# Finishing the prompt's rows inside the expert loop instead of behind it (hybrid decoder step, one core)

## The reference, cut to what matters

```python
g_idx = top_k(softmax(t @ rw1 + rb1), 1)               # one of 4 groups
v2, e_idx = top_k(logits of the 4 experts in it, 2)    # two of its experts
gates = one_hot(4 * g_idx + e_idx) * softmax(v2) * p_top
hid = silu(t @ w_gate[e]) * (t @ w_up[e]) * gates
out = sum over the two experts of hid @ w_down[e]      # hidden width 256
x = x + g2 * out                                       # x: the residual row
y = x * rsqrt(mean(x * x) + EPS) * final_norm_g        # both groups
```

## Time and profile before

| | us |
|---|---|
| median of 3 runs (1165.39 to 1166.51) | 1165.52 |
| the profiled execution's own time | 1166.91 |
| its span | 1165.1 |
| PE busy in it | 1075.8 (92%) |
| POOL busy in it | 312.9 (27%) |
| mean granted clock of TensorE | 0.974 |

### The profile page before, as it was taken

One profiled execution on the slowest core, in us unless ns is written; L12 is line 12 of the kernel. 1 busy time (PEld: TensorE's weight loads), 2 busy tenths in 40 slices (PEclk: granted clock), 3 DMA queues, 4 the chain that ended last, 5 costly groups with the idle time before them and its releaser, 6 DMA issues. The chain is left out here.

```text
span 1165.1 us, 18015 instructions
## 1 busy us (share of the span) xinstructions
PE 1075.8 (92%) x5413; PEld 806.9 (69%) x5414; DVE 765.8 (66%) x1256; ACT 516.1 (44%) x732; POOL 312.9 (27%) x370
## 2 busy tenths in 40 slices
PE   3799999999797989999999989999999999999992
PEld 2357777776465668787787646888888788888860
DVE  5557475747579954378887788555777555555375
ACT  5134252422333225446665243544566455544373
POOL 0046272626141000030000003333334433333244
PEclk9799999999989999999999999999999999999996
DMA  9933656567774459386766557897799877775597
GB/s 281 316 109 101 190 158 198 154 180 246 222 156 162 137 160 250 148 226 215 248 222 217 163 217 253 238 294 216 216 272 271 219 212 220 222 208 113 111 358 306
DMA packets 165460, 244.75 MB, mean 210 GB/s; under 512 B 65327, under 2 KB 122831, under 8 KB 161255
## 3 DMA queue, kind: packets, MB, share of 16 engines
q1 hardware_dynamic: 135065, 167.54, 45.0%
q0 software_dynamic: 17040, 57.87, 19.0%
q10 hardware_dynamic: 13302, 18.66, 4.6%
HBM read 169.36 MB, written 75.84 MB: 210 GB/s over the span
## 5 line engine op out<-in xcount | busy, mean ns | idle before, releaser
L126 PE MATMUL experts_psGU<-weights_we_hi,experts_x_hi 128*128 (+1 forms) x344 | 141.2, 410 | 2.1 <-DVE experts_x_lo L2714 1.0
L128 PE MATMUL experts_psGU<-weights_we_lo,experts_x_hi 128*128 (+1 forms) x344 | 136.0, 395 | 0.0
L127 PE MATMUL experts_psGU<-weights_we_hi,experts_x_lo 128*128 (+1 forms) x344 | 136.0, 395 | 0.0
L2540 POOL DMA_INDIRECT acc_d<-experts_o_sb,experts_to_col x40 | 71.0, 1776 | 209.2 <-DMA acc_d<-experts_o_sb,experts_to_col 109.5
L126 PE MATMUL front_psM<-front_hT_hi,front_w_hi 128*128 128x512 f32 x256 | 106.7, 417 | 0.9 <-DVE front_hT_lo L1043 0.9
L127 PE MATMUL front_psM<-front_hT_hi,front_w_lo 128*128 128x512 f32 x256 | 101.7, 397 | 0.0
L2733 DVE TENSOR_TENSOR experts_o_sb<-experts_psD,experts_g2r 128x1024 f32<-128x1024 f32 x43 | 52.7, 1225 | 74.5 <-PE experts_psD L128 74.5
L128 PE MATMUL front_psM<-front_hT_lo,front_w_hi 128*128 128x512 f32 x256 | 101.2, 395 | 0.0
L126 PEld LDWEIGHTS experts_psGU<-weights_we_hi,experts_x_hi 128*128 128x128 f32 x344 | 64.7, 188 | 20.9 <-issue 6.4
L128 PEld LDWEIGHTS experts_psGU<-weights_we_lo,experts_x_hi 128*128 128x128 f32 x344 | 64.6, 188 | 15.7
L2704 DVE TENSOR_TENSOR weights_we_lo<-weights_we_raw,weights_we_hi (+1 forms) x64 | 75.5, 1220 | 0.0
(11 more groups left out here) (530 smaller groups left out, 2522.3 us busy)
## 6 DMA issues: line engine op xcount, KB each, us to landing
front_raw<-in_w_ada SPq DMA_DIRECT2D x24, 1024.0 KB, 14.2
weights_we_raw<-in_exp_w_gate SPq DMA_DIRECT2D x16, 1024.0 KB
weights_we_raw<-in_exp_w_up SPq DMA_DIRECT2D x16, 1024.0 KB
weights_wd_raw<-in_exp_w_down SPq DMA_DIRECT2D x16, 1024.0 KB
front_xraw<-in_x_prompt SPq DMA_DIRECT2D x4, 2048.0 KB, 10.9
part_d<-middle_ev ACTq DMA_DIRECT2D x16, 512.0 KB, 3.8
middle_xt<-in_x_prompt SPq DMA_DIRECT2D x16, 512.0 KB, 4.8
middle_part<-part_d SPq DMA_DIRECT2D x16, 512.0 KB, 5.6
```

Source lines behind the costliest of these rows:

```text
L126: pe.matmul(out, l_hi, r_hi, start=start, stop=False)
L127: pe.matmul(out, l_lo, r_hi, start=False, stop=False)
L128: return pe.matmul(out, l_hi, r_lo, start=False, stop=stop)
L2540: pool.indirect_dma_start(acc_d, bass.IndirectOffsetOnAxis(tc[:, u, :], 0), osb[:, u, :], None, compute_op=ALU.add).then_inc(added, 16)
```

## The change

**Last slots are marked.** Routing gives a slot's gate a negative sign where it is the row's last: nine small POOL operations form the signs, DVE waits for them (`signs`), and after the sort takes the sign off again into `R.last`. POOL then builds `R.rows`, four indices per slot: the row to fetch, the row to add to (out of bounds for a last slot of the prompt), the row to fetch a sum from and the row to store to (both out of bounds for every other slot, and for padding).

**POOL's step.** Its order is new: `sums(t-4)` (the scatter-add without last slots, and behind it a gather-add from `acc_d` onto `osb` for last slots only), then `gather(t)`, then `store(t-6)`, which stores finished rows to the output, then waits for the transfers of the iteration before, `columns` (copies the next four indices), and `power(t-4)`, which raises the mean square to -0.5.

**ACT and DVE.** ACT gets `row_squares(s-2)` in each step, ahead of the weight splits. DVE gets `root_step(s-3)`, three operations on 128x1 that refine the power, and `row_norm(s-3)`, 128x1024. `g2r` has one buffer instead of two.

**Behind the loop** the 8 pairs of blocks, their loads and stores and the flags for them are gone; three late tiles and the samples are left, and some of their sums move from PE to DVE.

The diff, cut to its core:

```diff
-    def gather(self, pool, R, h2_d, t, u):
-        pool.tensor_copy(self.ic[:, u, :], R.idx[:, bass.ds(t, 1)]).then_inc(self.ic_ok, 1)
-        pool.wait_ge(self.ic_ok, t + 1)
-        pool.sem_inc(self.fence, 1)
-        pool.indirect_dma_start(self.xg[:, u, :], None, h2_d, bass.IndirectOffsetOnAxis(self.ic[:, u, :], 0)
+    def columns(self, pool, R, t, u):
+        pool.tensor_copy(self.cols[:, u, :], R.rows[:, bass.ds(t, 1), :].rearrange("p a n -> p (a n)")).then_inc(self.ic_ok, 1)
+    def gather(self, pool, h2_d, t, u):
+        pool.indirect_dma_start(self.xg[:, u, :], None, h2_d, bass.IndirectOffsetOnAxis(self.cols[:, u, 0:1], 0)
                                 ).then_inc(self.xg_in[u], 16)
...
+                if j == 0:
+                    dve.wait_ge(signs, 9)
                 gated = dve.tensor_tensor(A[:, 1, r], A[:, 0, r], b2(gt[:], NCOL), ALU.mult)
...
+            def sums(t, u):
+                pool.wait_ge(oev, OEV0 + t + 1)
+                pool.sem_inc(fence, 1)
+                if not isinstance(t, int) or t:
+                    pool.wait_ge(added, 16 * t)
+                    pool.sem_inc(freed, 1)
+                pool.sem_inc(fence, 1)
+                pool.indirect_dma_start(acc_d, bass.IndirectOffsetOnAxis(W.cols[:, u, 1:2], 0), osb[:, u, :], None,
+                                        bounds_check=TOK - 1, oob_is_err=False, compute_op=ALU.add).then_inc(added, 16)
+                pool.indirect_dma_start(osb[:, u, :], None, acc_d, bass.IndirectOffsetOnAxis(W.cols[:, u, 2:3], 0),
+                                        bounds_check=TP - 1, oob_is_err=False, compute_op=ALU.add).then_inc(acc_in[u], 16)
+            def power(t, u):
+                pool.wait_ge(mean_ok, MEAN0 + t)
+                pool.sem_inc(fence, 1)
+                pool.tensor_tensor(fss[:, u, 2:3], fss[:, u, 1:2], half[:], ALU.pow).then_inc(powers, 1)
+            def store(t, u, to):
+                pool.wait_ge(normed, NORM0 + t + 3)
...
             with pool.Fori(6, last + 1, 2) as t:
                 for d in range(2):
+                    pool.wait_ge(W.ic_ok, t + d + 1)
+                    pool.sem_inc(fence, 1)
+                    sums(t + d - 4, d)
                     pool.wait_ge(xt_ps, t + d - 1)
-                    W.gather(pool, R, h2_d, t + d, d)
-                    scatter(t + d - 4, d)
+                    pool.sem_inc(fence, 1)
+                    W.gather(pool, h2_d, t + d, d)
+                    store(t + d - 6, d, W.cols[:, d, 3:4])
+                    n, v = t + d - 1, 1 - d
+                    pool.wait_ge(xg_in[v], 8 * n + 16 - 8 * v)
...
+                    W.columns(pool, R, n + 2, v)
+                    power(t + d - 4, d)
...
+            def row_squares(t, u):
+                act.wait_ge(acc_in[u], 8 * t - 8 * u + 16 + ACC0)
...
+                act.activation(junk[:], osb[:, u, :], ACT.Square, scale=1.0 / 32, accum_out=fss[:, u, 0:1]).then_inc(fsq, 1)
+                act.wait_ge(fsq, FSQ0 + t + 3)
+                act.activation(fss[:, u, 1:2], fss[:, u, 0:1], ACT.Identity, bias=eps[:]).then_inc(mean_ok, 1)
...
+            def row_norm(t, u):
+                dve.wait_ge(fstep, STEPS * t + 2 * STEPS + 3)
+                dve.wait_ge(y_out[u], 8 * t - 8 * u + YOUT0)
+                dve.scalar_tensor_tensor(out=fo[:, u, :], in0=osb[:, u, :], scalar=fss[:, u, 5:6], in1=F.gn[:],
+                                         op0=ALU.mult, op1=ALU.mult).then_inc(normed, 1)
```

More of the change, by code:

```diff
@@ L2422, in experts @@
         SHARED = [(1, 0), (2, 0), (2, 1)]
-        PAIR = 2 * D * 4
-        homes = [(n, i * PAIR) for n in ("we_raw", "we_hi") for i in range(ROW_PAIRS // 2)]
-        rows = [k.over(f"rows{g}", [P, 2, D], homes[g][0], F32, homes[g][1]) for g in range(ROW_PAIRS)]
+        g2s = k.over("g2s", [TS, D], "we_raw")
         fix = k.over("late_rows", [P, LATE, D], "wd_raw")
@@ L2543, in expert_pool @@
             for t in range(2, 6):
+                W.columns(pool, R, t, t % 2)
+                pool.wait_ge(W.ic_ok, t + 1)
+                if t >= 4:
+                    sums(t - 4, t % 2)
                 pool.wait_ge(xt_ps, t - 1)
-                W.gather(pool, R, h2_d, t, t % 2)
+                W.gather(pool, h2_d, t, t % 2)
                 if t >= 4:
-                    scatter(t - 4, t % 2)
+                    power(t - 4, t % 2)
+                if t < 5:
+                    pool.wait_ge(xg_in[1 - t % 2], 8 * (t - 1) + 16 - 8 * (1 - t % 2))
@@ L2565, in expert_pool @@
                                         ).then_inc(late_in[d], 16)
+            store(end - 2, 0, last_to[:, 0, :])
             pool.wait_ge(late_in[0], 16)
@@ L2631, in squares @@
+            def squares(n):
+                if n == LATE_A:
+                    act.wait_ge(fsq, FSQ0 + end + 2)
+                if n < LATE_C:
+                    act.wait_ge(own_sum, n + 1)
+                elif n == LATE_C:
+                    act.wait_ge(c_sum, 1)
                 else:
                     act.wait_ge(s_x3, 1)
-                for r, x in enumerate(unit(n)):
-                    if r not in blocks:
-                        continue
-                    if n != ORDER[0] or r:
-                        act.wait_ge(sq, SQ[n] - len(unit(n)) + r)
-                    act.activation(junk[0:x.shape[0], :], x, ACT.Square, accum_out=part(n, 0)[:, r:r + 1]).then_inc(sq, 1)
+                if n:
+                    act.wait_ge(sq, n)
+                x = unit(n)
+                act.activation(junk[0:x.shape[0], :], x, ACT.Square, accum_out=part(n, 0)).then_inc(sq, 1)
@@ L2664, in expert_act @@
                     silu(s, u)
-                    gate_rows(s - 1, 1 - u)
+                    gate_rows(s - 1)
+                    row_squares(s - 2, u)
                     with act.If((code & 1) > 0):
@@ L2676, in expert_act @@
             silu(end + 1, 1)
-            gate_rows(end, 0)
+            gate_rows(end)
+            row_squares(end - 1, 1)
             with act.If((code & 1) > 0):
@@ L2683, in expert_act @@
             hidden_hi(end + 1)
-            squares(ORDER[0], (0,))
             silu(end + 2, 0)
-            gate_rows(end + 1, 1)
-            squares(ORDER[0], (1,))
-            act.wait_ge(eps_ok, 1)
-            root(ORDER[0])
+            gate_rows(end + 1)
             hidden_hi(end + 2)
-            gate_rows(end + 2, 0)
-            for n in ORDER[1:]:
+            gate_rows(end + 2)
+            for n in ORDER:
                 squares(n)
@@ L2732, in out, with root_step @@
                 dve.wait_ge(freed, FREED0 + t - 1)
-                dve.tensor_tensor(osb[:, u, :] if to is None else to, psD[:], g2r[:, u, :], ALU.mult).then_inc(oev, 1)
+                if to is None:
+                    dve.wait_ge(normed, NORM0 + t + 1)
+                dve.tensor_tensor(osb[:, u, :] if to is None else to, psD[:], g2r[:], ALU.mult).then_inc(oev, 1)
             ch = Chain(dve, last_c)
+            def root_step(t, u):
+                v, y0, w, h, y = [fss[:, u, j:j + 1] for j in range(1, 6)]
+                dve.wait_ge(powers, POW0 + t)
+                dve.scalar_tensor_tensor(out=w, in0=y0, scalar=y0, in1=v, op0=ALU.mult, op1=ALU.mult).then_inc(fstep, 1)
+                dve.wait_ge(fstep, STEPS * t + 2 * STEPS + 1)
+                dve.tensor_scalar(h, w, -0.5, 1.5, ALU.mult, ALU.add).then_inc(fstep, 1)
+                dve.wait_ge(fstep, STEPS * t + 2 * STEPS + 2)
+                dve.tensor_tensor(y, y0, h, ALU.mult).then_inc(fstep, 1)
@@ L2821, in expert_dve @@
                     x_lo_of(s + 1, 1 - u)
+                    root_step(s - 3, 1 - u)
                     hidden(s, u)
+                    row_norm(s - 3, 1 - u)
                     out(s - 1, 1 - u)
@@ L2832, in expert_dve @@
             x_lo_of(end + 2, 0)
+            root_step(end - 2, 0)
             hidden(end + 1, 1)
+            row_norm(end - 2, 0)
             out(end, 0)
-            late_parts()
             with dve.If((code & 1) > 0):
@@ L2841, in expert_dve @@
             hidden_lo(end + 1)
-            late_flags()
+            root_step(end - 1, 1)
             hidden(end + 2, 0)
+            row_norm(end - 1, 1)
             kept_rows()
@@ L2846, in expert_dve @@
             hidden_lo(end + 2)
-            store_rows()
-            norm(0)
-            norm(1)
+            late_sums(1, psB, b_sum)
             out(end + 2, 0, osb3[:])
-            for n in ORDER[2:]:
-                if n == LATE_C:
+            dve.wait_ge(oev, OEV0 + end + 3)
+            late_sums(2, psC, c_sum)
+            for n in ORDER:
+                if n == SAMPLES:
                     sample_sum()
```

302 lines of the change are left out of this document (152 added, 150 removed).

## The result

The changed kernel takes 1248.47 us (median of 4 runs, 1246.28 to 1250.94) against 1165.45 before (4 runs, 1165.03 to 1166.51): a ratio of 1.0711, 95% interval 1.0685 to 1.0738. The profiled execution spans 1248.2 us against 1165.1, so 83.1 us more are to be found.

What follows compares the result with a forecast made beforehand. PE was taken to bound the loop and DVE's order the stretch behind it. Loop +20 and behind it -9.8 gave +10.2 on 1166.9, 1177.1, or 1175.7 on the median's scale; forecast 1175.0, range 1157 to 1198.

Steps and rivals of the forecast that it cites:

- The loop, +20 predicted: Tile loop: POOL's longer cycle loses 36 us, 16 of it forgiven, leaving +20, between 0 and 57.
- I let each of the twelve bursts be forgiven 1.3.: Tile loop: slack absorbs 1.3 us of lateness at each of twelve loads, 16 us in all.
- Quiet ones: POOL's cycles without a load: 10.0 us, ends 9.1 and 11.6, against a beat of 9.5, so each loses 0.5.
- Beside a load: POOL's twelve cycles beside loads: 13.1 to 14.0 us full, 1.6 off for unmoved rows, 11.5 taken, each losing 2.0.
- the same lateness as above and shares its 2.6 of slack: ACT's row_squares ahead of the weight splits: no separate loss; without that cover up to 1.5 us in each of sixteen steps.
- The Trainium skill's fit: Gather-add in POOL's cycle: 2.0 us plus bytes at 436 GB/s gives 3.2, a cycle of 8.1 and the beat kept.
- The gather's slack of 0.65: Gather third in POOL's step: 0.65 us left of 10.8 before PE's turn waits for its rows.
- Routing and start: POOL's nine sign operations, 3.2 us, are covered, and building R.rows lies behind the first gathers: nothing lost.
- Behind the loop, -9.8 predicted: After the tile loop: fewer operations in DVE's order end the last norm at 1142.4 instead of 1152.23, -9.8 us.
- The store that follows it stays as it is: Program's end: the store behind the last norm is unchanged, with no term in the sum.
- B: Tile loop keeps its beat, scatters 9.5 us apart or less: 1156 to 1160, chance 0.23.
- C: Loop cycles heavier, left-out rows costing as much as moved ones, no burst forgiven, 57 or more: 1191 to 1215, chance 0.14.

Runs made afterwards that it cites:

- run 13: Changed kernel with DVE's low parts of the weights made for 32 columns only: 1219.23 us, ratio 1.046.
- run 1: Changed kernel with only POOL's power moved, directly behind the next tile's scatter: 1233.4 us, ratio 1.058.
- Run 2: Changed kernel with only the gather moved, in front of the scatter: 1295.87 us, ratio 1.112.
- run 3: Changed kernel with only ACT's squares moved, behind the weight splits of the same step: 1239.64 us, ratio 1.063.
- run 4: Changed kernel with power moved behind the next scatter and gather moved in front of the scatter: 1236.44 us, ratio 1.061.
- run 5: Changed kernel with power late, gather first and ACT's squares behind the weight splits: 1206.52 us, ratio 1.037.
- run 14: Kernel before the change, without the four stores of its last two pairs of blocks: 1161.81 us, ratio 0.9986.
- run 8: Changed kernel with all the gather-add's indices out of bounds, so it moves no row: 1207.00 us, ratio 1.037.
- run 10: Changed kernel with squares in the next step, power behind next gather-add, gather first, root_step behind hidden, third gather issued from R.idx: 1167.81 us, ratio 1.0028.
- run 11: Kernel of run 10 with the loop's twelve loads cut to one partition each: 1161.46 us, ratio 0.9976.
- run 12: Kernel of run 10 with POOL's copy of the next indices moved ahead of the store: 1171.32 us, ratio 1.0057.
- run 9: Changed kernel with the gather-add replaced by a transfer of 4 bytes on the same queue: 1195.12 us, ratio 1.027.

## Why the prediction was wrong

The direction was right; 1175 with a range to 1198 was not, against 1248.47.

**The loop, +20 predicted, +97.9 measured.** This is the step that failed, in three places.
- *"I let each of the twelve bursts be forgiven 1.3."* Nothing is forgiven. I held two clocks against each other, PE's beat of 9.5 and POOL's cycle, and let POOL catch up between bursts. With quiet cycles above 9.5 it never catches up: PE runs at POOL's pace, and each cycle's whole excess counts. By my own terms it should have been 27 x 0.5 + 12 x 2.0 = 38. That is 18 of the 78 us that are missing.
- *The cycles.* Quiet ones are 10.9, predicted 10.0: the landing 7.6 instead of 7.0, the power 0.57 and the restart behind it 1.0 (1.4 predicted for both), ACT's part 1.69 instead of 1.63. That is 27 x 0.9 = 25 more. Beside a load they are 14.8, predicted 11.5: the landing at 11.7 instead of 8.5. That is 12 x 3.3 = 40 more, the largest of the three. (Together they are 83 where 78 are missing, since the count over cycles gives 101 for the loop's 97.9.) My 1.6 off for rows that are not moved had nothing to stand on: the range that I had worked out for full tiles, 13.1 to 14.0, was too low as well. The gather-add's issue comes up to 3.6 us long, beside DVE's splits (run 13). (The quiet cycle's lower end was also added up wrongly: 6.1 + 1.63 + 0.2 + 1.0 is 8.9 and not 9.1, which changes nothing.)
- *The squares.* I wrote that their lateness is "the same lateness as above and shares its 2.6 of slack". Runs 1 to 5 show that it is a chain of its own: with POOL's one shortened only 15 us come back, with both of POOL's edits 12, and with the squares moved as well 42.

The Trainium skill's fit of a transfer (section "Anatomy of one DMA — SWDGE (gpsimd) path" of "DMA: Bandwidth & Descriptors") would have led further off: its cycle of 8.1 us stands against 10.9 here.

**The gather's slack of 0.65** was right as a sign: PE waits 34.9 us for gathered rows. Run 2 shows that the place behind the sums is still the better one as long as POOL's chain sets the pace. Once the power or the squares are moved it isn't free: a gather's landing stands once in the changed kernel's chain between 735 and 1190 us, 10 us in all, but takes 65 us of run 1's and 94 us of run 3's.

**Routing and start, "Nothing" predicted, +4.5 measured.** The nine operations on signs are free: the product that waits for them runs at 688.02, where it ran at 688.33. What failed is the sentence on building `R.rows`. It stands ahead of the third tile's gather, which moved from 708.46 to 713.59, and its rows came late for PE, which waited 2.6 us for them. POOL's and PE's timelines of the changed kernel:

```profile
713.59 2.67 POOL L2075 DMA_INDIRECT weights_xg<-h_d,weights_idx_cols  x1 [0.57 <-POOL weights_idx_cols L2071]
```

```profile
723.36 0.33 PE L2940 MATMUL experts_psX<-all_ident,weights_xg 128*128 128x128 f32 x1 [2.63 <-DMA weights_xg<-h_d,weights_idx_cols]
```

**Behind the loop, -9.8 predicted, -9.7 measured** from the 41st `out` to the last norm. That it fits so closely is partly luck. DVE's operations behind the last `out` took 14.7 us, where I had 15.2. The last `out` ended 18.4 after the 41st began, where I had 17.7 at most: a norm at 1219.67 took 3.30 instead of 1.28, beside a sum of full width on POOL, and the 42nd `out` came 12.1 after the 41st instead of 9.5.

**"The store that follows it stays as it is": 0 predicted, -9.6 measured.** I called the end "bound by DVE's order", though the earlier trace rows gave its DMA share as 0.84. It was the landing of POOL's last store and the drain behind it that ended the program, until 1164.9, both off the chain that I followed from the last norm; SP's store had landed at 1157.9. Four of the stores are 3.3 us of it (run 14). The store that I called unchanged lands in 2.9 us instead of 5.6. No run parts the rest. This term went the other way and hid a tenth of the loop's error.

**The rivals.** B is refuted: no cycle is under 9.76. C named the right kind, a heavier cycle and stretched issues, and was still 33 us short. Its reason, that left-out rows cost as much as moved ones, isn't borne out: with none moved 41 us come back (run 8). It too was worked out from cycles of 11 and 14 and counted only excesses over 9.5 in 40 steps. Its sum of 57 was made with a quiet cycle of 10.0, against its own 11; with its own numbers, 12 x 4.5 + 28 x 1.5 = 96, it would have had the time.

What stays open: in the kernel of run 10 the loop is still about 23 us longer than before. Loads are 6 of it (run 11), POOL's copy none (run 12). POOL's scatters there have a median of 2.6 us and the longest 3.69, DVE waits 33.5 us for POOL's power, and both point at the chain from power over norm to `out`. No run parts them. A part that I had no term for is PE's clock. From the first `out`'s end to the 41st's, before and in run 10:

```profile
728.41:1110.70 382.29, 381.38 (x1842) 311.20 (x1841) 226.38 (x232) 195.67 (x230) 134.90 (x160) 1.00 0.77 215
727.27:1132.99 405.72, 390.04 (x1842) 312.91 (x1841) 296.57 (x391) 249.98 (x350) 308.41 (x236) 0.99 0.74 206
```

The same 1842 matmuls are busy 8.7 us longer. In run 4's kernel it can be seen how: PE stands still from 919.6 to 926.3 us, its granted clock is then 0.50 (1.2 GHz) from 926.4 to 929.7, with 8 matmuls in 3.3 us, and 1.00 again after that. In run 5 the same matmuls are busy 400.7 us, which is 19 of the 56 us that its loop loses. In the changed kernel they are busy 406.1, but there PE is off the chain nearly everywhere.

## What to carry to other kernels

When a producer's loop is given a wait for its own result, sum that loop's whole cycle, quiet and disturbed, and hold it against the beat of the engine that bounds. If the quiet cycle is longer, nothing is forgiven and every excess counts in full; if it is shorter, only bursts longer than the slack do. Then look for further chains through the same transfer or queue on other in-order engines, and move all of them together, since shortening one may show little: 15 and 9 us alone, 75 of the loop's 98 when all waits were moved far enough behind the landing. At a program's end, look at which queue's last landing and drain end it, and not only at the last arithmetic.

## What the hardware showed

An accumulating indirect transfer's issue on POOL takes 1.6 us, or up to 3.69 beside DVE's subtractions of two SBUF operands for the weights' low parts. In the kernel before, the 12 scatters whose issue lay, by the two timelines, beside only such DVE operations as read one operand from PSUM took 1.60 to 1.65. Of the 28 beside low parts 7 took 2.13 to 3.69, one 1.66 and 20 took 1.60 or 1.61. In run 13, with those operations short, no accumulating transfer's issue passes 1.67. The Trainium skill states a rule in "SBUF — State Buffer", section "SBUF: two separate sides": a DVE operation with two SBUF inputs and a GpSimd operation that reads SBUF exclude each other on a shared pair of ports, and whichever starts first holds it. The long issues agree with that. The 20 short ones, most of which lay wholly beside a low part, show that it isn't all, and no run here tells which of the issue's accesses is held up.

A gather-add with no row to move still ties up 1.6 to 3.6 us of issue (run 8), and its landing releases the squares: runs 8 and 9 differ by 12 us.

POOL's drain at the end takes 3.8 to 5.6 us. In the changed kernel it lay under another queue's landing, and before it ended the program.
